# A third of the gates' projection in attention's steps, with cache keys and values single-buffered

## The reference

```python
h = _rms_norm(x, norm_mix_pre)
p = h @ w_in
qa, ka, va, qkv_b, z_b, a_b, b_b, gate_a, gate_b = jnp.split(p, split_at, axis=-1)
# prompt: each chunk of 64 frames attends to itself and the 8 chunks before it
sc = jnp.einsum('blhd,bmhd->bhlm', qc, kb) * scale + bias
p = jax.nn.softmax(sc, axis=-1)
out = jnp.einsum('bhlm,bmhd->blhd', p, vb)
# sample: each of the 8 streams attends to 512 cached rows and its own 16
# then the gated delta rule on qkv_b, and
merged = jax.nn.sigmoid(gate_a) * y_a + jax.nn.sigmoid(gate_b) * y_b
x = x + _rms_norm(merged @ w_out, norm_mix_post)
# then the MLP: f = square(relu(h2 @ w_up)) @ w_down
```

## Time and profile before

| what | value |
|---|---|
| median of 3 runs | 2033.51 us (2029.74 to 2036.84) |
| profiled execution, first to last instruction | 2028.7 us |
| TensorE, VectorE, ScalarE, GpSimd busy | 96%, 37%, 31%, 29% of the span |
| mean granted TensorE clock | 0.988 |
| norm and first slabs / projection / attention | to 68 / 68 to 595 / 595 to 785 us |
| delta rule / tail | 785 to 1004 / 1004 to 2029 us |

### The profile page before, as it was taken

The page is one execution under the profiler, slowest core; times in us unless marked ns, Lnnn a source line. Parts: engine busy times, 40 slices in busy tenths (PEclk is TensorE's granted clock), DMA queues, the critical chain, the costliest instruction groups (busy, mean ns, idle before and its releaser), DMA issues. The chain is left out here.

```text
span 2028.7 us, 34282 instructions
## 1 busy us (share of the span) xinstructions
PE 1945.0 (96%) x14050; PEld 1759.9 (87%) x14050; DVE 746.8 (37%) x1482; ACT 634.4 (31%) x1283; POOL 590.6 (29%) x456
## 2 busy tenths in 40 slices
PE   7999999999998888899799999999999999999998
PEld 7899999999994566678699879999999999999997
DVE  5211777111125664565553182222222222222225
ACT  5101222100016664344443245222222222222222
POOL 3111111111132002543354144333333333333333
PEclk9999999999998998999899999999999999999999
DMA  4322223522227213131253232111111111111114
GB/s 119 108 89 88 76 88 118 209 88 88 88 97 238 92 64 84 44 96 39 62 158 105 104 125 88 47 43 42 42 42 42 42 42 42 42 42 42 42 60 169
DMA packets 159273, 169.22 MB, mean 83 GB/s; under 512 B 14187, under 2 KB 130043, under 8 KB 159150
## 3 DMA queue, kind: packets, MB, share of 16 engines
q1 hardware_dynamic: 152814, 141.52, 22.7%
q10 hardware_dynamic: 6336, 25.96, 3.2%
HBM read 126.84 MB, written 40.55 MB: 83 GB/s over the span
## 5 line engine op out<-in xcount | busy, mean ns | idle before, releaser
L2369 DVE TENSOR_TENSOR t_acc<-t_acc,t_B 128x512 f32<-128x512 f32 x252 | 173.3, 688 | 538.6 <-PE t_B L2475 538.6
L116 PE MATMUL i_ps<-x_hi,i_w_lo 128*128 128x384 f32 x1008 | 337.5, 335 | 0.0
L116 PE MATMUL i_ps<-x_hi,i_w_hi 128*128 128x384 f32 x1008 | 337.2, 335 | 0.0
L116 PE MATMUL i_ps<-x_lo,i_w_hi 128*128 128x384 f32 x1008 | 337.2, 335 | 0.0
L2462 PE MATMUL t_B<-t_merged_hi,t_wm_lo 128*128 128x384 f32 x768 | 256.9, 335 | 1.0 <-POOL t_wm_lo L2052 1.0
L2462 PE MATMUL t_B<-t_merged_lo,t_wm_hi 128*128 128x384 f32 x768 | 256.6, 334 | 0.0
L2462 PE MATMUL t_B<-t_merged_hi,t_wm_hi 128*128 128x384 f32 x768 | 256.6, 334 | 0.0
L106 POOL TENSOR_TENSOR i_w_lo<-i_w_raw,i_w_hi 128x1024 fp32r<-128x1024 f32 x44 | 105.4, 2395 | 433.4 <-ACT i_w_hi L101 433.4
L2052 POOL TENSOR_TENSOR t_wm_lo<-t_raw,t_wm_hi 128x1024 fp32r<-128x1024 f32 x49 | 118.8, 2425 | 295.9 <-ACT t_wm_hi L2127 295.9
L116 PEld LDWEIGHTS i_ps<-x_lo,i_w_hi 128*128 128x128 f32 x1008 | 189.8, 188 | 0.0
L116 PEld LDWEIGHTS i_ps<-x_hi,i_w_lo 128*128 128x128 f32 x1008 | 189.7, 188 | 0.0
(11 more groups left out here) (344 smaller groups left out, 3465.9 us busy)
## 6 DMA issues: line engine op xcount, KB each, us to landing
proj<-i_out ACTq DMA_DIRECT2D x44, 576.0 KB, 2.8
i_w_raw<-in_w_in SPq DMA_DIRECT2D x44, 512.0 KB, 3.9
t_raw<-in_w_up SPq DMA_DIRECT2D x32, 512.0 KB, 4.2
t_raw<-in_w_down SPq DMA_DIRECT2D x32, 512.0 KB, 3.6
t_gates<-proj SPq DMA_DIRECT2D x48, 192.0 KB, 2.7
a_k_cache<-in_cache_attn_k SPq DMA_DIRECT2D x8, 1024.0 KB, 6.1
a_v_cache<-in_cache_attn_v SPq DMA_DIRECT2D x8, 1024.0 KB, 5.3
d_c<-proj SPq DMA_DIRECT2D x3, 1536.0 KB, 7.6
```

Source lines behind the costliest of these rows:

```text
L116: last = pe.matmul(out, a[s][:, c, :], b[:, c, tokens], start=k == 0, stop=k == n - 1)
L2369: dve.tensor_tensor(a, a, B[(ND * j + d) % 4][:, :], ALU.add).then_inc(added, 1)
```

## The change

The last token group (tokens 768 to 1151) of the 16 gates' slabs leaves the projection, whose last 16 slabs run two groups of three. It is computed in attention, by TensorE in steps 4 to 67, four steps to a slab, "part" 0 to 3: in parts 0 and 1 three matmuls (one chunk) before the turn and six after it, in part 2 three and three, in part 3 none. ScalarE makes the high half in two pieces at the end of its parts 2 and 3 of the slab before, GpSimd subtracts after both, ScalarE copies the sums out of PSUM at the end of part 2, SP loads and stores. For the room, `x_hi` and `x_lo` are three tiles each of which the last stays, the cached keys, values and turned keys have one buffer instead of two, and the scores of two units share three PSUM banks instead of four, which frees the bank `GP`. The first conv columns, whose SBUF the slabs use, are loaded after the last gates. The diff, cut to its core:

```diff
@@ slab_products
-def slab_products(pe, w, s, x_hi, x_lo, out, chunks, tokens):
+def slab_products(pe, w, s, x_hi, x_lo, out, chunks):
...
@@ stage_in_proj, TensorE
-            with pe.Fori(1, HALF) as i:
+            def slabs(a, b, groups):
...
+                        for g in range(groups):
...
+            slabs(1, GATES_AT, NTG)
+            slabs(GATES_AT, HALF, NTG - 1)
@@ stage_in_proj, VectorE
-            plain(NZ // 2 + 2, HALF)
+            plain(GATES_AT, HALF, NTG - 1)
@@ stage_attention, buffers
-        kc = [sb(f"k_cache{i}", [P, 4, AW]) for i in range(2)]
-        vc = [sb(f"v_cache{i}", [P, 4, AW]) for i in range(2)]
-        kt = [sb(f"k_cache_t{i}", [P, 4, REACH]) for i in range(2)]
+        kc, vc = sb("k_cache", [P, 4, AW]), sb("v_cache", [P, 4, AW])
+        kt = sb("k_cache_t", [P, 4, REACH])
-        S = [c.enter_context(nc.psum_tensor(f"a_S{i}", [P, 1024], F32)) for i in range(2)]
+        SB = c.enter_context(nc.psum_tensor("a_S", [P, 1536], F32))
+        NGATE, GSTEPS, GSTART = NSLAB[1], 4, 4
+        w_raw = nc.alloc_sbuf_tensor_at("a_gate_w", [P, DC, P], F32, offset=env.c_at)
+        w_hi, w_lo = ([nc.alloc_sbuf_tensor_at(f"a_gate_w_{kind}{i}", [P, DC, P], F32R, offset=w_at[i] + k * SLAB)
+                       for i in range(2)] for k, kind in enumerate(("hi", "lo")))
+        def gate_part(st):
+            n = st - GSTART
+            return divmod(n, GSTEPS) if 0 <= n < NGATE * GSTEPS else (None, None)
@@ stage_attention, SP
+            def load_gate_w(n):
+                if n:
+                    sp.wait_ge(w_lo_made, n)
+                sp.dma_start(w_raw[:, :, :], w_in[:, :, COL_GATE + n * P:COL_GATE + (n + 1) * P]).then_inc(w_landed, 16)
+            load_k(0)
+            load_v(0)
...
+            load_gate_w(0)
...
+            for st in range(STEPS):
+                n, part_ = gate_part(st)
+                if part_ == 0 and n + 1 < NGATE:
+                    load_gate_w(n + 1)
+                if part_ == 2 and n:
+                    store_gate(n - 1)
+                b, h = divmod(st, STEP)
+                if h == 7 and b + 1 < NB:
+                    load_k(b + 1)
+                if h == 5 and 0 < b < NB:
+                    load_v(b)
@@ stage_attention, GpSimd, after the bias copies
+            for n in range(NGATE):
+                pool.wait_ge(w_hi_made, 2 * n + 2)
+                pool.tensor_tensor(w_lo[n % 2][:, :, :], w_raw[:, :, :], w_hi[n % 2][:, :, :].bitcast(F32), ALU.subtract
+                                   ).then_inc(w_lo_made, 1)
@@ stage_attention, ScalarE
+            def gate_high(n, half):
+                act.wait_ge(w_landed, 16 * n + 16)
+                if n >= 2:
+                    act.wait_ge(g_prod, n - 1)
+                if n == 1:
+                    act.wait_ge(saved, 16 * 6)
+                cs = slice(4 * half, 4 * half + 4)
+                act.activation(w_hi[n % 2][:, cs, :], w_raw[:, cs, :], ACT.Copy).then_inc(w_hi_made, 1)
...
+                if st in (1, 2):
+                    gate_high(0, st - 1)
+                n, part_ = gate_part(st)
+                if part_ in (2, 3) and n + 1 < NGATE:
+                    gate_high(n + 1, part_ - 2)
+                if part_ == GSTEPS - 2:
+                    gate_out(n)
@@ stage_attention, TensorE
+            def gates(n, cc):
+                if cc == 0:
+                    pe.wait_ge(w_lo_made, n + 1)
+                    if n:
+                        pe.wait_ge(g_free, n)
...
+                if n is not None and part_ < 3:
+                    gates(n, 3 * part_)
                 if 0 <= st - 3 < NU:
                     turn(st - 3)
+                if n is not None:
+                    for cc in range(3 * part_ + 1, min(3 * part_ + 3, DC)):
+                        gates(n, cc)
@@ scores_pair: for five key blocks the far columns first, one count for both heads
+                parts = ((0, 0, W), (1, 0, W)) if n < 5 else ((e, 512, W), (1 - e, P, W), (e, 0, 512), (1 - e, 0, P))
@@ scores_stream
-                pe.wait_ge(s_read, u - 1)
+                pe.wait_ge(s_read, u)
```

More of the change, by code:

```diff
@@ L115, in slab_products @@
         for a, b in ((w.lo, x_hi), (w.hi, x_lo), (w.hi, x_hi)):
-            last = pe.matmul(out, a[s][:, c, :], b[:, c, tokens], start=k == 0, stop=k == n - 1)
+            last = pe.matmul(out, a[s][:, c, :], b[:, c, :], start=k == 0, stop=k == n - 1)
             k += 1
@@ L290, in products @@
                 for cc in range(part * DC // 2, (part + 1) * DC // 2):
-                    for a, b in ((w.lo, env.x_hi), (w.hi, env.x_lo), (w.hi, env.x_hi)):
-                        last = pe.matmul(env.ps[NTG * sl + g][:, 0:TG], a[sl][:, cc, :], b[:, cc, tokens],
-                                         start=cc == 0 and a is w.lo, stop=cc == DC - 1 and a is w.hi and b is env.x_hi)
+                    for a, b in ((w.lo, env.x_hi[g]), (w.hi, env.x_lo[g]), (w.hi, env.x_hi[g])):
+                        last = pe.matmul(env.ps[NTG * sl + g][:, 0:TG], a[sl][:, cc, :], b[:, cc, :],
+                                         start=cc == 0 and a is w.lo, stop=cc == DC - 1 and a is w.hi and b is env.x_hi[g])
                 if part == 1:
@@ L427, in _ @@
                     store(act, i, s)
-            plain(NZ // 2 + 2, HALF - 1)
+            with act.Fori(GATES_AT, HALF - 1) as i:
+                for s in range(2):
+                    split_hi(act, w, i + 1, s)
+                    evacuated(i, s)
+                    store_gates(i, s)
             for s in range(2):
                 evacuated(HALF - 1, s)
-                store(act, HALF - 1, s)
+                store_gates(HALF - 1, s)
             act.wait_ge(env.v_in, 16)
@@ L478, in plain @@
                         dve.wait_ge(sent[s], 16 * i + 16)
-                        for g in range(NTG):
+                        for g in range(groups):
                             m = 3 * (2 * i + s) + g
@@ L652, in keys_of, with scores_at, stream_scores @@
             return b, h, n, (b - n + 1) * P
+        def scores_at(u, a, z):
+            first = 0 if u % 2 == 0 else 1536 - (keys_of(u)[2] * P if prompt(u) else KEYS)
+            return SB[:, first + a:first + z]
+        def stream_scores(u):
+            return (SB[:, 0:REACH], SB[:, REACH:KEYS]) if u % 2 == 0 else (SB[:, 1024:1536], SB[:, 1024 - P:1024])
         def turned_p(u):
@@ L887, in soft @@
                     b = u // STEP
+                    cached, own = stream_scores(u)
                     if b == 0:
@@ L975, in scores_pair @@
                 b, h, n, k0 = keys_of(u)
-                for a in range(0, n * P, 512):
-                    z = min(n * P, a + 512)
-                    for i in range(2):
-                        half = slice(AD * i, AD * i + AD)
-                        last = pe.matmul(S[(u + i) % 2][:, a:z], q[half, h // 2, b * P:(b + 1) * P],
-                                         k[half, h // 2, k0 + a:k0 + z], start=True, stop=True)
-                        if z == n * P:
-                            last.then_inc(s_made, 1)
+                W = n * P
+                e = u % 2
+                parts = ((0, 0, W), (1, 0, W)) if n < 5 else ((e, 512, W), (1 - e, P, W), (e, 0, 512), (1 - e, 0, P))
+                for j, (i, a, z) in enumerate(parts):
+                    half = slice(AD * i, AD * i + AD)
+                    if j == 3:
+                        pe.wait_ge(far_scores, (b - 4) * (AH // 2) + h // 2 + 1)
+                    last = pe.matmul(scores_at(u + i, a, z), q[half, h // 2, b * P:(b + 1) * P],
+                                     k[half, h // 2, k0 + a:k0 + z], start=True, stop=True)
+                    if n < 5:
+                        last.then_inc(s_made, 1)
+                    elif j == 0:
+                        last.then_inc(far_scores, 1)
+                if n == 5:
+                    last.then_inc(s_made, 2)
             def scores_stream(u):
-                pe.wait_ge(s_read, u - 1)
-                ps, b = S[u % 2], u // STEP
+                pe.wait_ge(s_read, u)
+                b = u // STEP
+                cached, own = stream_scores(u)
                 pe.wait_ge(tk_read, side["K", 4 * b + 3] + 1)
@@ L990, in scores_stream @@
                 for j in range(4):
[L991 removed]
+                    pe.matmul(cached[2 * TS * j:2 * TS * (j + 1), :], qd[b % 2][:, j, :], kt[:, j, :],
                               start=True, stop=True)
                 for j in range(4):
[L994 removed]
+                    last = pe.matmul(own[2 * TS * j:2 * TS * (j + 1), :], qd[b % 2][:, j, :], k[:, j, TP:T],
                                      start=True, stop=True)
@@ L1049, in values_stream @@
                 last.then_inc(av_made, 1)
+            def gates(n, cc):
[3 more added lines that the diff above has]
+                        pe.wait_ge(g_free, n)
+                h, lo, xh, xl = w_hi[n % 2], w_lo[n % 2], env.x_hi[NTG - 1], env.x_lo[NTG - 1]
```

(6 more changed lines are left out.)

121 lines of the change are left out of this document (71 added, 50 removed).

## The result

The changed kernel takes **2103.7 us** (median of 4 runs, 2100.3 to 2107.4) against 2033.2 before (2029.7 to 2036.8): a ratio of **1.035, 95% interval 1.033 to 1.037**. Slower; 2102 was forecast.

A forecast was written before the change was run, and what follows sets the result against it. TensorE, busy 1945.0 of 2028.7 us, was taken to bound the kernel. The terms -66.8 + 66.8 - 16 + 55 + 5 + 24 = +68 us, added to the median 2033.5, gave 2102 us, range 2064 to 2130.

The forecast's parts named there:

- Removed and added products, -66.8 and +66.8: 384 gates' matmuls leave the projection, saving 66.8 us, and cost 66.8 us again on TensorE in attention.
- Filled waits, -16: In attention, moved matmuls fill three quarters of TensorE's 22 us of waits: -16 us, bounds 0 and 22.
- The low halves of slabs 1 to 15, +55: In attention, TensorE waits for GpSimd's low half, made from ScalarE's late high half: +55 us, bounds 30 and 70.
- By place: Step's place in its block of nine sets TensorE's other work, hence each slab's wait, 2.0 to 4.5 us.
- ScalarE's lateness and the products' wait: In attention, ScalarE late after a short part 2, three slabs, 1.4 us each; products' wait 0.1 to 0.2 per slab.
- The first slab, +5: At attention's step 4, the first slab's subtraction stands behind GpSimd's mask copies, so TensorE waits: +5 us.
- The clock, +24: TensorE's sixteen new pauses in attention lower its granted clock, 1.5 us each: +24 us, bounds 0 and 27.
- Rival 1: TensorE's clock stays at its upper level through the pauses in attention: 2078 us, chance 0.15.
- Single buffers 0: In attention, single-buffered keys and values cost 0, since six steps are 16 us against 6.9 us to land.
- side engines 0: In attention, ScalarE's added halves and copies, about 25 us over about 220, cost 0 beyond the low halves' chain.
- The hold of VectorE by GpSimd: In attention, GpSimd's subtraction holds VectorE's scaling of scores up to 2.4 us: cost 0; 38 us if all on path.
- The sum: Over the whole kernel, all terms together: +68 us, giving 2102 us, slower.

The follow-up runs named there:

- fourth: Changed kernel with only 2 narrow products of each slab's 24 made in attention, all waits and side work kept: 2054.4 us, ratio 1.010.
- ninth, experiment 9: Changed kernel with one product a slab, from activations alone, and no TensorE wait for low halves; side work kept: 1988.8 us, ratio 0.979.
- seventh experiment: Changed kernel with low halves made and awaited in two pieces, and all slabs starting in step 6 instead of 4: 2017.7 us, ratio 0.993.
- third experiment: Changed kernel with 15 dummy products ahead of the first product of slabs 1 to 15, filling the wait: 2079.5 us, ratio 1.022.
- first experiment: Changed kernel with ScalarE's high halves made one step earlier, in a slab's second and third step: 2034.2 us, ratio 1.001.
- sixth: Changed kernel with GpSimd making the low halves in two pieces, TensorE waiting for the second only before its fifth chunk: 2020.5 us, ratio 0.994.
- tenth: Changed kernel with GpSimd making each slab's subtraction twice and TensorE waiting for the second: 2146.6 us, ratio 1.056.
- second experiment: Changed kernel with the gates' last third back in the projection, single buffers, load order and layout kept: 2032.5 us, ratio 0.999.

## Why the prediction was right, and where its terms were off

- **Removed and added products, -66.8 and +66.8.** The projection ended 66.0 us earlier. The fourth and ninth experiments bear out that the products in attention are not the cost.
- **Filled waits, -16.** In the changed kernel turns and stream values wait 11 us less, hidden under the new wait. Seen by itself in the seventh experiment, where the new wait is nearly gone: 2033.5 - 2017.7 = 15.8 us. The agreement is partly luck, since that kernel also pays something for its first short steps.
- **The low halves of slabs 1 to 15, +55.** Measured 55.5, in 15 waits. The chain is the one that was followed. By place: 0 and 2 were put at 4.5 and came to 4.17 to 4.71; 4 and 6 at 3.3, all three 3.62; 7 at 3.4, came to 3.1 and 4.2; 5 at 3.2, came to 3.9. Places 1, 8 and 3 were put too low, at 2.0: 3.42 and 2.99, 2.39, 3.10. At the first of them the blocks are narrow, and turn, values and scores cover 1.9 us (610.62 to 612.50) instead of 3.2; at the others the cover was as forecast (3.0 to 3.7), but from the turn's start to the first product it took 5.4 to 6.8 us instead of 5.2 and 5.8. The places were put at 49 us together, and 6 were added for ScalarE's lateness and the products' wait; 3.9 of the 6.5 missing from 49 lie at these four. So the total fits better than its parts, which is partly luck.
- **The first slab, +5: measured 9.2. This step failed.** It took the scores at 617.41 for TensorE's step 4. In the trace of before the pairs' scores start at

```profile
610.42 0.49 PE L980 MATMUL a_S<-k,q 64*128 64x128 f32 x4 [0.69 <-ACT a_bias L810]
611.64 0.49 PE L980 MATMUL a_S<-k,q 64*128 64x128 f32 x4 [0.72 <-DVE a_nmax L884]
613.49 0.49 PE L980 MATMUL a_S<-k,q 64*128 64x128 f32 x4
```

  and these are steps 0, 2 and 4, so 617.41 is step 6. GpSimd's side was right: low half ready at 623.3 by the forecast, and in the changed kernel, where all comes 66 us earlier, at 557.13:

```profile
547.18 0.80 PE L1077 MATMUL a_S<-k,q 64*128 64x128 f32 x4
...
554.32 0.50 POOL L855 COPY a_bias_s<-a_bias_s 128x384 f32<-128x384 f32 x1
554.79 2.34 POOL L858 TENSOR_TENSOR a_gate_w_lo<-a_gate_w,a_gate_w_hi 128x1024 fp32r<-128x1024 f32 x1
```

  With 613.49 + 0.5 the same sum gives 623.3 - 614.0 = 9.3. In a row of like blocks one has to count from the first.
- **The clock, +24.** The third experiment gives 24.2 for 15 pauses. The term was drawn from one pause of 2.2 us in the tail, at 1.5 us for each of 16; that one case carried so far is partly luck. Rival 1, a clock that stays up, is out. Its premise, a clock of 1.00 in attention before, holds for 626 to 785 us; from 611 to 626 it was 0.66. Full clock lost in attention, in us, added up over stretches of 1 us, and how much of it lies inside TensorE's waits for the low half:

```
                       lost   inside the waits   outside
kernel before           5.1          -             5.1
changed kernel         41.0         9.4           31.6
first experiment        6.8         4.9            1.9
third                  10.2         4.3            5.9
sixth                   6.8         4.3            2.5
tenth                  66.5        27.2           39.3
```

  What is lost outside is what costs: against the changed kernel it is 25.7 less in the third (24.2 measured), 29.7 less in the first and 29.1 less in the sixth (29.1 and 30.1 measured beyond the waits themselves), and 7.7 more in the tenth (3.5 measured).
- **Single buffers 0, side engines 0.** The second experiment confirms the first. The second zero fits the changed kernel, and does not hold in general (experiment 9). The hold of VectorE by GpSimd is in the trace, off the path:

```profile
568.61 2.34 POOL L858 TENSOR_TENSOR a_gate_w_lo<-a_gate_w,a_gate_w_hi 128x1024 fp32r<-128x1024 f32 x1 [11.47 <-ACT a_gate_w_hi L900]
...
569.29 1.74 DVE L1002 TENSOR_SCALAR a_s<-a_s,a_rinv 128x128 f32<-128x128 f32 x1
```

  128 columns took VectorE 1.74 us, to the subtraction's end, where 640 columns took 0.55 with GpSimd idle (at 719.19). The Trainium skill, "SBUF — State Buffer", section "SBUF: two separate sides", has such a hold as an exclusive lock. The row agrees.
- **The sum.** With 9.2 for 5 and the clock of the third experiment it is -16 + 55.5 + 9.2 + 24 = 72.7, against 70.5 measured. The too small first slab was made up by other errors of a few us.

## What to carry to other kernels

Before work is moved into an engine's holes, follow the chain that feeds it through the other engines' queues, and compare its length with what the engine has to do meanwhile: here, in the trace, 4.8 to 7.2 us from the turn to the low half against 0.6 to 3.7 us of cover. If the chain is longer, don't give the move up, but start the chain a step earlier or hand its product over in pieces: either alone was worth 70 to 83 us here, and the pieces made the move pay, 2018 to 2021 us against 2033. And where TensorE pauses for as long as here, 2.4 us and more, count the pause twice: its length, and some 1.6 us for the clock. Pauses of 0.3 to 1.7 us, 13 of them in the first experiment, cost their length alone.

## What was not expected of the hardware

The clock can fall after a pause is over: four times it went down 0.6 to 1.3 us after TensorE had taken up work again, so the first matmul behind a pause does not show whether the pause cost clock. Nor does the length of a pause settle it alone: one of 2.39 us (to 689.23) was followed by a fall, one of 2.99 us (to 783.64) was not. Over all the price is steady, 24 to 30 us for the pauses of this kernel. And work can have a negative price: 39 us of useless products made the kernel 24 us faster.
